# One kernel change: gathering tokens per expert in the first quad of a mixture-of-experts stage

## The chip, the cores and the metric

One core of a Trainium2 chip. The metric is the device time of one execution in microseconds (us), median of several runs. Lower is better.

## The reference, cut to what matters

Two blocks run one after the other on 256 tokens of width 1024, in f32. The first has two hybrid attention layers and is not touched here. The second has two layers, each with an attention and a mixture of experts. Only the experts matter for the change: 32 experts in each layer, and each token goes to two of them.

```python
def hierarchical_moe(h, w_group, b_group, w_expert, b_expert, w_gate, w_up, w_down):
    ...
    def expert_block(args):
        xb, e = args
        return (jax.nn.silu(xb @ w_gate[e]) * (xb @ w_up[e])) @ w_down[e]
    ...
    ys = ys * row_gate[:, None].astype(ys.dtype)
    out = jnp.zeros((N + 1, D), ys.dtype).at[row_tok].add(ys)[:N]
```

`w_gate[e]` and `w_up[e]` are 1024 x 512, `w_down[e]` is 512 x 1024, in f32: 2 MB each, 192 MB in a layer. Every expert's weights are read from memory once.

## The kernel before, in words

**Stages.** The program runs two hybrid layers, then for i = 0 and 1 an attention (`neighbourhood` or `grouped`), the router and the experts of layer i. Each engine has its own instruction list, and they meet at semaphores. Two names say how PSUM's eight banks are handed over: `filled(...)` is raised by TensorE (PE) when a result stands in a bank, `drained(...)` by the engine that has read it. PE's `begin(b, ...)` waits until the last result in bank b is drained.

**The router.** VectorE (DVE) works out the groups, the experts, the position of each token within its expert (`R_PM`) and the gate values. `select(i, q)` (line 1580) builds the 0/1 matrices `SEL` that say which token stands in which of the 32 places of each of the four experts of quad q. After `select(i, 0)` DVE writes the gate values (`gates`), the overflow mask and the counts (lines 1644 to 1653), and then reads one or two results of the conditioning projection (`extract`, lines 1654 and 1655).

**The experts.** 32 experts are eight quads of four, `for q in range(NQ)`. In each quad:
- `gather(q)`: the tokens of all four experts are gathered by matmuls. The stationary operand is a 128 x 128 block of the normalized tokens `XH`, the moving operand is `SEL` of the quad, 128 columns (4 experts x 32 places). There are 8 blocks of columns x 2 blocks of tokens = 16 matmuls, which the trace records as 32 (each f32 matmul has two records). Banks 0 and 1 take the results, and ScalarE (ACT, bank 0) and DVE (bank 1) write them, scaled and shifted, to `XG`. `gather(0)` stands ahead of the loop, `gather(q + 1)` after the last expert of quad q.
- for each expert j of the quad (lines 889 to 915) the gate product (m = 0) and the up product (m = 1), 64 records each with a 128 x 32 block of `XG` as the stationary operand, four of them side by side in the array (line 898). Then ACT takes silu of the gate, DVE multiplies by up (`AA`), PE transposes the product (`hidden(j)`, bank 4) and DVE copies it to `AT`. `hidden(j - 1)` stands after expert j, `hidden(3)` after the loop.
- after expert 0 only (the others leave with `continue`): DVE multiplies `SEL` by `gates` to `GS`, PE transposes that in bank 4 (`gsT`, line 911), DVE copies it to `GST` (line 1707), and builds the next quad's `SEL`. In layer 1, quad 0, `second_gates(i, 1)` (line 667 on PE) follows.
- `down(0)` and `down(1)` (line 932): 64 records each of 128 x 512; then `combine` (line 942) adds the quad's rows to the output with `GST`.

**The weights.** All weights pass through nine slots of 2 MB (`ring` has five, `AR` four). `plan()` assigns every piece to a slot; `PIECE` holds a piece's slot and how often the slot was filled, `BEFORE` the piece that was there. SyncE (SP) issues the loads in the order of use, at line 2325, each after the old piece's `DONE`: the gate product's last matmul for a gate piece, the up product's for an up piece, and `filled("dn", i, q, 1)`, the end of `down(1)`, for a down piece. By the plan, the first down piece of quad 0 (`("dn", i, 0, 0)`) takes slot 7; the other three take the slots of expert 0's gate, expert 0's up and expert 1's gate; the next five pieces (gate and up of experts 4 and 5, gate of expert 6) take those of expert 1's up to expert 3's up. The piece after them, expert 6's up, takes slot 7, and so waits for quad 0's `down(1)`. SP's list is in order: all later loads stand behind it.

**GpSimd (POOL)** adds the layer norm's rows to `X` (`finish`, line 2186), beside the first experts.

Of the kernel before, what the change touches and what calls it, by code (L numbers as in the profile page):

```python
# [130 lines left out]
def program(nc, A, out):  # L131
    with ExitStack() as ctx:
# [175 lines left out]

        def plan():
            age, held, holds, now = list(range(RING + EXTRA)), [0] * (RING + EXTRA), {}, [RING + EXTRA]  # L310

            def put(name, among, at=None):
                s = min(range(among), key=lambda i: age[i])
                age[s] = now[0] if at is None else at
                now[0] += at is None
                held[s] += 1
                PIECE[name], BEFORE[name] = (s, held[s]), holds.get(s)
                holds[s] = name

            n_ada = itertools.count()  # L320
            for l in range(DEPTH):
                for f in LOADS[l]:
                    if f == "ada":
                        put(("ada", next(n_ada)), RING)
                    else:
                        put(("out", l, f) if f in (0, 1) else ("in", l, f), RING)
            for *f, when in NA_LOADS:
                put(("wo", 0, f[1]) if f[0] == "wo" else ("ada", f[1]) if f[0] == "ada" else ("qkv", 0, *f), RING, when)
            for k, when in enumerate((486, 487, 510, 505)):
                age[RING + k] = when  # L330
            now[0] = 1000
            for i in range(DEPTH):
                if i:
                    base = now[0]
                    for *f, when in GQA_LOADS:
                        put(("ada", f[1]) if f[0] == "ada" else ("wo", 1, f[1]) if f[0] == "wo" else ("qkv", 1, *f), RING, base + when)
                    for k, when in enumerate((95, 96, 128, 122)):
                        age[RING + k] = base + when
                    now[0] = base + 200
                for q in range(NQ):  # L340
                    for j in range(4):
                        for m in range(2):
                            put(("gu", i, 4 * q + j, m), RING + EXTRA)
                    for k in down_pieces(q):
                        put(("dn", i, q, *k), RING + EXTRA)
# [68 lines left out]
        def _(eng):  # L414
# [453 lines left out]
            def experts(i):  # L868
                def gather(q):
                    for b in range(2):  # L870
                        o = begin(b, "xg", i, q, b)
# [8 lines left out]
                gather(0)  # L880
                for q in range(NQ):
# [7 lines left out]
                    for j in range(4):  # L889
                        o = begin(2 + j % 2, "gu", i, q, j)  # L890
                        for m in range(2):
# [3 lines left out]
                            for c in range(NC):  # L895
                                pe.wait_ge(*drained("xg", i, q, c // 4))
                                for f in range(4):
                                    ins = eng.matmul(o[32 * f:32 * f + 32, 128 * m:128 * m + 128],  # L898
                                                     XG[u][:, c, 32 * j:32 * j + 32], w[:, c, f::4],
                                                     start=c == 0, stop=c == NC - 1)  # L900
                            if not m:
                                DONE[name] = pe.step(ins)
                        end(ins, "gu", i, q, j)
                        DONE[name] = filled("gu", i, q, j)
                        if j:
                            hidden(j - 1)
                            continue
                        o = begin(4, "gsT", i, q)
                        pe.wait_ge(sem("gs"), 8 * i + q + 1)
                        for t in range(NT):  # L910
                            ins = turn(o[:, 128 * t:128 * t + 128], GS[u][:, t, :])
                        end(ins, "gsT", i, q)
                        if i and not q:
                            second_gates(i, 1)
# [98 lines left out]
        def _(eng):  # L1013
# [575 lines left out]
            def router(i):  # L1589
# [53 lines left out]
                select(i, 0)  # L1643
                for t in range(NT):
                    v.step(tt(gates[:, t, :].rearrange("p (g e) -> p g e", g=4), bcast(ohg[:, t, :], 2, 8),
                              bcast(oh1[:, t, :], 1, 4), ALU.mult))
                v.chain()
                v.step(stt(over[:, :, :], pm, CAP + 0.5, gates[:, :, :], ALU.is_gt, ALU.mult))
# [5 lines left out]
                for n in (23,) if i else (18, 19):  # L1654
                    extract(n)

            def experts(i):
# [15 lines left out]
                gather(0)  # L1673
                for q in range(NQ):
# [8 lines left out]
                    for j in range(4):  # L1683
                        w = j % 2
                        bk = bank("gu", i, q, j)
                        v.wait_ge(*filled("gu", i, q, j))
# [6 lines left out]
                        if j:  # L1693
                            hidden(j - 1)
                            continue
# [10 lines left out]
                        v.wait_ge(*filled("gsT", i, q))  # L1706
                        free(eng.tensor_copy(GST[u], bank("gsT", i, q)[:, 0:256]), "gsT", i, q)
                        if q + 1 < NQ:
                            select(i, q + 1)
                    hidden(3)  # L1710
# [106 lines left out]
            for i in range(DEPTH):  # L1817
# [4 lines left out]
                router(i)  # L1822
                experts(i)
# [3 lines left out]
        def _(eng):  # L1827
# [293 lines left out]
            def experts(i):  # L2121
                def gather(q):
# [13 lines left out]
                gather(0)  # L2136
                for q in range(NQ):
                    for j in range(4):
                        n = 32 * i + 4 * q + j
# [6 lines left out]
                        if i and not (q or j):  # L2146
                            second_gates(i, 1)
# [169 lines left out]
        def _(eng):  # L2317
            sp = Engine(eng, sem("sp"))

            def load(dst, src, *name):  # L2320
                held = BEFORE[name]
                if held:
                    sp.wait_ge(*DONE[held])
                s, _ = PIECE[name]
# [192 lines left out]
```

## Time and profile before

| | us |
|---|---|
| runs shown (three) | 1564.13, 1565.1, 1570.44 |
| median | 1565.1 |
| profiled execution, its time | 1563.89 |
| profiled execution, its span (first to last instruction) | 1562.2 |
| PE busy | 1389.6 (89%) |
| DVE busy | 571.8 (37%) |
| ACT busy | 215.0 (14%) |
| POOL busy | 88.4 (6%) |
| moved by DMA | 533.32 MB |

The span is 1.7 us shorter than the profiled execution's own time. PE is the TensorE matmul row and PEld its weight loads, which overlap it; a busy PE is not a PE at its peak. "PEclk" is the TensorE clock that was granted, as a share of 2.4 GHz, and "DMA" the mean busy share of the core's 16 DMA engines. The expert stage of layer 0 runs from 484 to 942 us of the span, that of layer 1 from 1093 to 1551 us.

### The profile page before, as it was taken

The page shows a single profiled execution, that of the slowest core. Times are in us where ns is not written, and L with a number is a line of the kernel's source. Part 1 is how long each engine was busy: PE and PEld are TensorE (multiplying, and loading weights), DVE is VectorE, ACT ScalarE, POOL GpSimd, SP SyncE. Part 2 cuts the span into 40 slices and gives each one's busy share as a digit, 9 for nine tenths or more (in the row PEclk, how much of TensorE's full clock was granted, in tenths as well). Part 3 has the DMA queues.
Part 4 walks back from the last instruction along what each step waited for, and adds up shares of the span by engine and source line. Part 5 has one row for each costly group of instructions (what it writes and reads, how often), then busy time and mean ns, then how long its engine had stood idle before and what let it go on. Part 6 is the DMA issues. An engine that isn't in the chain of part 4 may idle for free.

```text
span 1562.2 us, 28408 instructions
## 1 busy us (share of the span) xinstructions
PE 1389.6 (89%) x12800; PEld 883.6 (57%) x12800; DVE 571.8 (37%) x1254; ACT 215.0 (14%) x574; POOL 88.4 (6%) x95
## 2 busy tenths in 40 slices
PE   7999999999998999779879788878999797897795
PEld 4885478578886556346446344457655453463451
DVE  3696469655745111101101115684222011011013
ACT  2230123022332000000000002442100000000000
POOL 3100111000003000000000001100200000000000
PEclk9999999999999999889899898999999998998997
DMA  9656845768768999999999998257999999999995
GB/s 345 216 197 233 291 164 198 275 220 288 280 278 340 411 426 426 428 426 426 427 426 428 427 376 320 89 201 282 374 413 426 428 426 427 427 426 427 425 415 201
DMA packets 96856, 533.32 MB, mean 341 GB/s; under 512 B 5184, under 2 KB 7424, under 8 KB 73168
## 3 DMA queue, kind: packets, MB, share of 16 engines
q1 hardware_dynamic: 92992, 519.40, 82.6%
q0 software_dynamic: 3728, 11.95, 2.2%
q8 instruction: 105, 1.72, 0.4%
q14 instruction: 31, 0.25, 0.0%
HBM read 530.28 MB, written 1.05 MB: 340 GB/s over the span
## 4 chain that ended last, share of the span: by engine, by line
PE 65%; DMA 24%; DVE 4%; SPq 4%; ACT 1%; issue 1%; DVEq 0%; ACTq 0%
PE bk L433 28%; PE bk L898 16%; DMA ring<-in_moe_w_down 15%; DMA AR<-in_moe_w_down 9%; PE bk L932 8%; PE bk L614 4%; PE bk L942 4%; SPq L2325 3%; PE bk L429 3%; DVE AR L1017 2%; PE bk L643 1%; PE bk L658 1%; ACT AR L1831 1%; DMA ring<-in_w_in 1%; DVE AR L1025 0%
## 5 line engine op out<-in xcount | busy, mean ns | idle before, releaser
L898 PE MATMUL bk<-ring,AR 128*32 128x128 f32 x4480 | 268.6, 409 | 0.1
L1017 DVE TENSOR_TENSOR AR<-bk,AR 128x128 f32<-128x128 f32 (+2 forms) x106 | 41.3, 390 | 521.6 <-ACT AR L1831 455.6
L898 PE MATMUL bk<-AR 128*32 128x128 f32 x3712 | 223.0, 409 | 0.0
L898 PEld LDWEIGHTS bk<-ring,AR 128*32 128x32 f32 x4480 | 175.7, 127 | 80.9 <-DVE X L1017 4.5
L433 PE MATMUL bk<-ring,AR 128*128 128x256 f32 (+2 forms) x736 | 214.1, 449 | 6.3 <-ACT AR L1831 2.6
L932 PE MATMUL bk<-ring,AR 128*32 128x512 f32 x608 | 159.4, 704 | 51.9 <-DMA ring<-in_moe_w_down 51.1
L1831 ACT ACTIVATE AR<-bk 128x512 f32<-128x512 f32 (+4 forms) x178 | 72.1, 422 | 948.2 <-PE bk L898 774.1
L898 PEld LDWEIGHTS bk<-AR 128*32 128x32 f32 x3712 | 145.5, 127 | 68.5 <-DVE X L1017 4.5
L433 PEld LDWEIGHTS bk<-ring,AR 128*128 128x128 f32 x736 | 140.9, 194 | 73.7 <-issue 56.6
L932 PE MATMUL bk<-AR 128*32 128x512 f32 x416 | 150.9, 709 | 27.8 <-DMA AR<-in_moe_w_down 27.8
L433 PE MATMUL bk<-AR,ring 128*128 128x256 f32 (+1 forms) x832 | 170.5, 364 | 1.7 <-DVE AR L1022 1.4
L433 PEld LDWEIGHTS bk<-AR,ring 128*128 128x128 f32 x832 | 147.5, 190 | 21.6 <-issue 3.4
L932 PEld LDWEIGHTS bk<-ring,AR 128*32 128x32 f32 x608 | 35.4, 126 | 130.1 <-DMA ring<-in_moe_w_down 71.6
L1017 DVE TENSOR_TENSOR AR<-bk,mpart 128x512 f32<-128x512 f32 x32 | 22.1, 692 | 220.9 <-PE bk L932 220.9
L429 PE MATMUL bk<-cst,AR 128*128 128x128 f32 (+1 forms) x356 | 63.9, 293 | 41.5 <-DVE AR L1017 24.1
L1025 DVE SCALAR_TENSOR_TENSOR mpart<-ring,ccol,mpart 128x512 f32<-128x512 f32 x126 | 98.7, 784 | 4.5
L429 PEld LDWEIGHTS bk<-cst,AR 128*128 128x128 f32 (+1 forms) x356 | 41.6, 143 | 79.7 <-issue 55.8
L932 PEld LDWEIGHTS bk<-AR 128*32 128x32 f32 x416 | 32.0, 126 | 73.4 <-DMA AR<-in_moe_w_down 39.7
L433 PE MATMUL bk<-AR 128*128 128x128 f32 (+1 forms) x536 | 72.1, 295 | 0.2
L433 PEld LDWEIGHTS bk<-AR 128*128 128x128 f32 x536 | 67.1, 202 | 4.4 <-issue 2.3
L942 PE MATMUL bk<-AR 128*128 128x512 f32 x128 | 59.7, 606 | 3.3 <-DVE AR L1017 3.3
L1017 DVE TENSOR_TENSOR X<-X,bk 128x512 f32<-128x512 f32 x64 | 44.0, 688 | 40.1 <-PE bk L614 23.9
(152 smaller groups left out, 954.1 us busy)
## 6 DMA issues: line engine op xcount, KB each, us to landing
ring<-in_moe_w_gate SPq DMA_DIRECT2D x36, 2048.0 KB, 28.6
ring<-in_moe_w_up SPq DMA_DIRECT2D x34, 2048.0 KB, 25.0
ring<-in_moe_w_down SPq DMA_DIRECT2D x34, 2048.0 KB, 33.6
AR<-in_moe_w_up SPq DMA_DIRECT2D x30, 2048.0 KB, 29.9
AR<-in_moe_w_gate SPq DMA_DIRECT2D x28, 2048.0 KB, 26.3
ring<-in_ada_w SPq DMA_DIRECT2D x24, 2048.0 KB, 11.0
AR<-in_moe_w_down SPq DMA_DIRECT2D x22, 2048.0 KB, 33.6
ring<-in_w_in SPq DMA_DIRECT2D x12, 2048.0 KB, 12.6
```

The lines of the kernel that those rows point to most:

```text
L429: return eng.transpose(o, a, ident[0:k, 0:k])
L433: ins = eng.matmul(o, l, r, start=i == 0, stop=i == len(pairs) - 1)
L614: ins = eng.matmul(o[:, :], BIG[:, x, OUTS[m] + 128 * t:OUTS[m] + 128 * t + 128], w[:, 2 * m + x, :], start=k + x == 0, stop=k + x == 4)
L643: ins = eng.matmul(o[b][:, a * nk:(a + 1) * nk], g["q"][h][:, t * 128:(t + 1) * 128], g["k"][h][:, 0:nk], start=True, stop=True)
L658: ins = eng.matmul(o[64 * b:64 * b + 64, 128 * x:128 * x + 128], g["v"][2 * x + b][kt], ET[j % 2][:, (2 * b + x) * nkt + kt, :], start=kt ...
L898: ins = eng.matmul(o[32 * f:32 * f + 32, 128 * m:128 * m + 128], XG[u][:, c, 32 * j:32 * j + 32], w[:, c, f::4], start=c == 0, stop=c == N ...
L932: ins = eng.matmul(o[32 * j:32 * j + 32, :], AT[u][:, j, 32 * f:32 * f + 32], w, start=f == 0, stop=f == 3)
L942: end(eng.matmul(o[:, :], GST[u][:, 128 * t:128 * t + 128], YS[:, 512 * n:512 * n + 512], start=True, stop=True), "cb", i, q, n, t)
L1017: return eng.tensor_tensor(o, a, b, op)
L1025: return eng.scalar_tensor_tensor(out=o, in0=a, scalar=s, in1=b, op0=op0, op1=op1)
L1831: return eng.activation(o, a, f, **kw)
L2325: eng.dma_start(dst, src).then_inc(sem(f"slot{s}"), 16)
```

## The change

In quad 0 of each layer every expert's tokens are gathered by themselves: `gather(0, n)` runs the same 16 matmuls with the 32 columns of `SEL` that belong to expert n. `gather(0, 0)` stands ahead of the loop, `gather(0, j + 1)` between expert j's gate and up products. ACT and DVE empty the banks with `gather_first(n)`, 32 columns wide. DVE's end of the router (gates, overflow mask, counts) becomes `router_end`, and runs after `gather_first(0)`.

The load that refills the slot of the first gate piece (it brings the down weights of expert 1) is issued as two loads of 1 MB: the first after half of the gate product (semaphore `half`), the second after all of it.

In all quads, the product of `SEL` and `gates`, and the next quad's `select`, move on DVE from after expert 0 to after expert 2, and the transpose `gsT`, its copy and `second_gates(i, 1)` from after expert 0 to after expert 3. `extract` moves from the router to quad 0, after expert 2.

```diff
@@ plan()
+        def first_gate(name):
+            return name in [("gu", i, 0, 0) for i in range(DEPTH)]
...
-                held[s] += 1
-                PIECE[name], BEFORE[name] = (s, held[s]), holds.get(s)
+                BEFORE[name] = holds.get(s)
+                held[s] += 2 if first_gate(BEFORE[name]) else 1
+                PIECE[name] = s, held[s]
@@ PE, experts(i)
-                def gather(q):
+
+                def gather(q, n=None):
                     for b in range(2):
+                        if n is not None:
+                            o = begin(b, "xe", i, n, b)
+                            pe.wait_ge(sem("xn"), 4 * i + 2)
+                            pe.wait_ge(sem("sel"), 8 * i + 1)
+                            for cc in range(4):
+                                ins = product(o[:, 32 * cc:32 * cc + 32],
+                                              [(XH[:, t, 128 * (4 * b + cc):128 * (4 * b + cc) + 128],
+                                                SEL[0][t][:, n, :]) for t in range(NT)])
+                            end(ins, "xe", i, n, b)
+                            continue
...
-                gather(0)
+                gather(0, 0)
...
-                                pe.wait_ge(*drained("xg", i, q, c // 4))
+                                pe.wait_ge(*(drained("xg", i, q, c // 4) if q else drained("xe", i, j, c // 4)))
...
+                                if first_gate(name) and c == NC // 2 - 1:
+                                    ins.then_inc(sem("half"), 1)
                             if not m:
                                 DONE[name] = pe.step(ins)
+                                if not q and j < 3:
+                                    gather(0, j + 1)
...
                         if j:
                             hidden(j - 1)
-                            continue
-                        o = begin(4, "gsT", i, q)
...
-                        if i and not q:
-                            second_gates(i, 1)
+                    o = begin(4, "gsT", i, q)
+                    pe.wait_ge(sem("gs"), 8 * i + q + 1)
...
+                    if i and not q:
+                        second_gates(i, 1)
                     hidden(3)
@@ DVE, router(i) and experts(i)
                 select(i, 0)
+                return ohg, oh1
+            def router_end(i, ohg, oh1):
...
+                def gather_first(n):
+                    v.wait_ge(*filled("xe", i, n, 1))
+                    for cc in range(4):
+                        c = 4 + cc
+                        ins = ts(XG[0][:, c, 32 * n:32 * n + 32], bank("xe", i, n, 1)[:, 32 * cc:32 * cc + 32],
+                                 COMB[:, 2 * i, 0, c:c + 1], ALU.mult, COMB[:, 2 * i, 1, c:c + 1], ALU.add)
...
-                gather(0)
+                gather_first(0)
+                router_end(i, *chosen)
...
+                        if not q and j < 3:
+                            gather_first(j + 1)
...
+                        if j != 2:
                             continue
...
-                        v.wait_ge(*filled("gsT", i, q))
-                        free(eng.tensor_copy(GST[u], bank("gsT", i, q)[:, 0:256]), "gsT", i, q)
                         if q + 1 < NQ:
                             select(i, q + 1)
+                        if not q:
+                            for n in (23,) if i else (18, 19):
+                                extract(n)
+                    v.wait_ge(*filled("gsT", i, q))
+                    free(eng.tensor_copy(GST[u], bank("gsT", i, q)[:, 0:256]), "gsT", i, q)
                     hidden(3)
@@ ACT, experts(i)
-                gather(0)
+                gather_first(0)
...
+                        if not q and j < 3:
+                            gather_first(j + 1)
...
-                        if i and not (q or j):
-                            second_gates(i, 1)
+                    if i and not q:
+                        second_gates(i, 1)
@@ SP, load(dst, src, *name)
+                if first_gate(held):
+                    h = dst.shape[1] // 2
+                    sp.wait_ge(sem("half"), held[1] + 1)
+                    eng.dma_start(dst[:, 0:h, :], src[:, 0:h, :]).then_inc(sem(f"slot{s}"), 16)
+                    sp.wait_ge(*DONE[held])
+                    eng.dma_start(dst[:, h:2 * h, :], src[:, h:2 * h, :]).then_inc(sem(f"slot{s}"), 16)
+                    return
```

## Rows read from the trace of the kernel before

**Rows 1.** Stretches: us, busy us of engines (instructions), then PEclk, DMA share, GB/s.
```profile
540.00:580.00 40.00, 37.99 (x570) 24.63 (x566) 5.33 (x18) 2.62 (x8) 0.00 (x0) 1.00 1.01 427
...
1150.00:1500.00 350.00, 302.22 (x3800) 172.88 (x3796) 52.67 (x138) 15.68 (x48) 0.59 (x1) 0.94 1.01 427
```

**Rows 2.** PE's waits in layer 0's experts: us in total, times, longest.
```profile
PE bk L932 <- DMA ring<-in_moe_w_down: 21.7, 7, 4.8
```

**Rows 3.** Order of time, DMA issues of SP in layer 0: start, us, engine, line.
```profile
493.68 10.40 SPq L2325 DMA_DIRECT2D ring<-in_moe_w_down  x3
...
522.96 0.33 SPq L2325 DMA_DIRECT2D AR<-in_moe_w_gate  x1
534.85 0.33 SPq L2325 DMA_DIRECT2D AR<-in_moe_w_up  x1
```

**Rows 4.** Stretches of 1 us around the restarts of DMA (columns as in 1).
```profile
492.00:493.00 1.00, 1.00 (x24) 0.69 (x20) 0.00 (x0) 0.00 (x0) 0.00 (x0) 1.00 0.02 8
...
535.00:536.00 1.00, 1.00 (x3) 0.40 (x3) 0.67 (x2) 0.00 (x0) 0.00 (x0) 1.00 0.88 262
536.00:537.00 1.00, 1.00 (x4) 0.41 (x3) 0.83 (x2) 0.00 (x0) 0.00 (x0) 1.00 0.72 229
...
1145.00:1146.00 1.00, 1.00 (x4) 0.49 (x3) 0.83 (x2) 0.00 (x0) 0.00 (x0) 1.00 0.43 147
```

**Rows 5.** Order of time: quad 1's gather, and the `down` after it.
```profile
524.05 3.74 PE L433 MATMUL bk<-AR 128*128 128x128 f32 x32
...
527.72 0.62 PE L932 MATMUL bk<-AR 128*32 128x512 f32 x1
```

**Rows 6.** Order of time: router logits, 36 moving columns, and the last record's length.
```profile
474.73 1.95 PE L433 MATMUL bk<-wr,AR 128*128 128x36 f32 x16
L433 PE MATMUL bk<-wr,AR x16: 271/279/279, 474.7 to 476.4; 128*128 128x36 f32 x16
```

**Rows 7.** Low clock: 32-column matmuls, the first gather, and the stretch in layer 0.
```profile
482.49 1.47 PE L433 MATMUL bk<-AR,ones 128*128 128x32 f32 x6
484.04 5.72 PE L433 MATMUL bk<-AR 128*128 128x128 f32 x32
481.00:488.00 7.00, 6.30 (x28) 6.20 (x29) 6.41 (x25) 0.61 (x4) 0.00 (x0) 0.52 1.02 410
```

**Rows 8.** Order of time, layer 0: expert 0, the `gsT` stop, expert 1.
```profile
489.70 7.59 PE L898 MATMUL bk<-ring,AR 128*32 128x128 f32 x128
...
499.50 0.41 PE L429 MATMUL bk<-cst,AR 128*128 128x128 f32 x2 [2.21 <-DVE AR L1017]
499.84 3.87 PE L898 MATMUL bk<-ring,AR 128*32 128x128 f32 x64
499.95 0.42 DVE L1707 COPY AR<-bk 128x256 f32<-128x256 f32 x1 [0.59 <-PE bk L429]
...
503.50 3.96 PE L898 MATMUL bk<-AR 128*32 128x128 f32 x64
```

**Rows 9.** The same place in layer 1.
```profile
1097.87 7.62 PE L898 MATMUL bk<-ring,AR 128*32 128x128 f32 x128
...
1107.32 0.41 PE L429 MATMUL bk<-cst,AR 128*128 128x128 f32 x2 [1.82 <-DVE AR L1017]
1108.71 3.88 PE L898 MATMUL bk<-ring,AR 128*32 128x128 f32 x64
```

**Rows 10.** Order of time, layer 0: the transpose after expert 3.
```profile
523.89 0.33 PE L429 MATMUL bk<-cst,AR 128*128 128x128 f32 x1 [0.74 <-DVE AR L1681]
```

**Rows 11.** Order of time: readers of the banks, and POOL beside them.
```profile
487.83 1.50 ACT L1831 ACTIVATE AR<-bk,cst 128x128 f32<-128x128 f32 x4 [5.76 <-PE bk L433]
493.15 5.85 POOL L2186 TENSOR_TENSOR X<-AR 128x1024 f32<-128x1024 f32 x2 [17.66 <-DMA AR<-in_ln_g]
497.75 0.29 DVE L1017 TENSOR_TENSOR AR<-bk,AR 128x128 f32<-128x128 f32 x1 [6.57 <-ACT AR L1831]
500.29 3.89 DVE L1017 TENSOR_TENSOR AR<-cst,AR 128x128 f32<-128x128 f32 x2
```

More of the change, by code:

```diff
@@ L906, in experts @@
                             hidden(j - 1)
-                            continue
-                        o = begin(4, "gsT", i, q)
[L909 to L912, printed above, removed]
-                        if i and not q:
-                            second_gates(i, 1)
+                    o = begin(4, "gsT", i, q)
+                    pe.wait_ge(sem("gs"), 8 * i + q + 1)
+                    for t in range(NT):
+                        ins = turn(o[:, 128 * t:128 * t + 128], GS[u][:, t, :])
+                    end(ins, "gsT", i, q)
+                    if i and not q:
+                        second_gates(i, 1)
                     hidden(3)
@@ L1647, in router @@
                 v.chain()
-                v.step(stt(over[:, :, :], pm, CAP + 0.5, gates[:, :, :], ALU.is_gt, ALU.mult))
+                v.step(stt(over[:, :, :], R_PM, CAP + 0.5, gates[:, :, :], ALU.is_gt, ALU.mult))
                 v.wait_ge(*filled("ct", i))
@@ L1653, in router, with experts @@
                 v.tell(eng.tensor_copy(cnt[:, NE:NE + 1], rt(388, 1)), sem("cnt"), i + 1)
-                for n in (23,) if i else (18, 19):
-                    extract(n)
-            def experts(i):
+            def experts(i, chosen):
+                def gather_first(n):
[4 more added lines that the diff above has]
+                                 COMB[:, 2 * i, 0, c:c + 1], ALU.mult, COMB[:, 2 * i, 1, c:c + 1], ALU.add)
+                        if cc == 3:
+                            free(ins, "xe", i, n, 1)
+                        else:
+                            v.step(ins)
                 def gather(q):
@@ L1821, in _ @@
                     neighbourhood()
-                router(i)
-                experts(i)
+                experts(i, router(i))
                 last_norm(i)
@@ L2121, in experts, with gather_first @@
             def experts(i):
+                def gather_first(n):
+                    s.wait_ge(*filled("xe", i, n, 0))
+                    for c in range(4):
+                        ins = act(XG[0][:, c, 32 * n:32 * n + 32], bank("xe", i, n, 0)[:, 32 * c:32 * c + 32], ACT.Identity,
+                                  bias=COMB[:, 2 * i, 1, c:c + 1], scale=COMB[:, 2 * i, 0, c:c + 1])
+                        if c == 3:
+                            free(ins, "xe", i, n, 0)
+                        else:
+                            s.step(ins)
                 def gather(q):
@@ L2321, in load @@
                 held = BEFORE[name]
+                s, _ = PIECE[name]
+                if first_gate(held):
[5 more added lines that the diff above has]
+                    return
                 if held:
                     sp.wait_ge(*DONE[held])
-                s, _ = PIECE[name]
                 eng.dma_start(dst, src).then_inc(sem(f"slot{s}"), 16)
```

## The prediction

> **What bounds the kernel now.** I read the stretches first. From 540 us on, with one exception per layer, the DMA engines are busy all of the time in the expert stages, at 427 GB/s [rows 1]. A stage whose loads run without a break ends when the last of them has landed, so what one edit is worth is: by how much does it move the moment from which the loads run without a break? The waits say the same from the other side: in layer 0's experts PE's longest sums of waits are `down` matmuls waiting for their weights (seven waits of 21.7 us in all on one kind of slot) [rows 2]. They are PE's slack, and no slack of the loads.
>
> The unbroken run begins late. SP's issues [rows 3] show why: expert 6's up goes to slot 7, which holds the first down piece, so its load (issued at 534.85) waits for quad 0's `down(1)`, and everything behind it in SP's list waits too. The issue before it was at 522.96. The loads queued by then had landed: 535 to 537 us moved 262 and 229 GB/s instead of 427, and layer 1 has the same hole at 1145 [rows 4]. There is an earlier hole at 492, where SP waits for the first gate's slot [rows 4], but only eight more pieces may be issued before `down(1)` ends, and they have all but landed when it does; filling that hole alone moves nothing. So the stage of each layer hangs on PE's list from the first gather to the end of quad 0's `down(1)`: what PE gains or loses there, the layer gains or loses. PE does not wait for a load in it.
>
> **The gathers.** Before, quad 0 has one gather of 32 records; after, four of 32 records each, since the 16 blocks of `XH` are loaded into the array for each expert anew and only the moving side shrinks, from 128 columns to 32. What does a record with few columns cost? In quad 1's gather the records come (3.74 - 0.28) / 31 = 0.112 us apart with 128 columns, and from its start to that of the next `down` it is 3.67 us [rows 5]. The router's logits have the same 128 x 128 stationary block and 36 columns: (1.95 - 0.28) / 15 = 0.111 us apart [rows 6]. So the spacing does not depend on the columns here, and a gather of 32 columns costs what one of 128 does. At the lower clock (granted 0.52 in that stretch, that is mostly 1.2 GHz) 32-column matmuls lie (1.47 - 0.40) / 5 = 0.214 us apart [rows 7] (0.40 is the length of one), twice as much. I take 3.67 us for each of the three added gathers, 11.0 us in each layer, because the nearest row is 36 columns wide and agrees. Bounds: 32 x 0.106 = 3.4 us if the spacing falls a little with the 4 columns fewer and the seam costs nothing (5% under the row of 36, my allowance), and 32 x 0.214 = 6.8 us if it runs wholly at 1.2 GHz.
>
> The rule of the Trainium skill, TensorE: Matmul & The Clock Gate, section "Back-to-back issue gap", would speak against this: it gives some 60 cycles (25 ns) for 1 to 64 columns. By it alone a 32-record gather would be 0.8 us. The same page's section "LDWEIGHTS (loading the stationary operand)" gives columns / 1.2 ns for the weight load, 107 ns for 128 columns, which the 0.111 us agree with. The first rule is a rival below.
>
> The first gather (5.72 us, from 484.04) [rows 7] is followed by expert 0 without a gap, at 489.70 [rows 8]. `gather(0, 0)` has as many loads at the same clock, so expert 0 starts when it did: 0. Bound: if the clock rises later than before, up to 32 x 0.214 + 0.3 - 5.72 = +1.4 us; downward 0.3 us. The bank readers get narrower, but they were hidden behind PE's own gather already.
>
> **The `gsT` stop.** Layer 0: expert 0's two products start 3.66 us apart (503.50 - 499.84, as for expert 1), so PE could start expert 1 at 489.70 + 7.32 = 497.02, and starts it at 499.84: 2.8 us, of which 2.21 are the wait for DVE's `GS` [rows 8]. They go: nothing stands between expert 0 and 1 any more. Layer 1: 1097.87 + 7.32 = 1105.19 against 1108.71: 3.5 us, with the second gates in it [rows 9].
>
> They come back in part after expert 3. PE waits there for DVE to copy the transpose of expert 2 before it may transpose expert 3, at 523.89 (0.74 us of wait) [rows 10]; all of these use bank 4. Now `gsT` takes that turn: from its start to the end of its copy 499.95 + 0.42 - 499.50 = 0.87 us [rows 8], some 0.9 with the hand-over, and only then expert 3's transpose. +0.9 us in layer 0. In layer 1 `second_gates` follows it, 1108.71 - 1107.32 = 1.4 us [rows 9]; its copy is within that: +1.4 us. Behind the transpose wait the next gather and both downs. In quads 1 to 7 the same move is a gain of under 1 us for PE, in a stretch in which the loads decide: 0.
>
> **What has cover.** `gather_first(j + 1)` on ACT and DVE runs while PE does expert j's up product, 3.66 us. ACT's four reads of 128 columns took 1.50 us [rows 11], at 32 they take no more. DVE's place beside POOL matters: two products of two SBUF operands took 3.89 us while POOL was at work, but one that reads a bank 0.29 us in the same time [rows 11]. `gather_first` reads a bank, so 0; if it were slowed like the others, 4 x 1.95 = 7.8 us less the 3.66 of cover and the 1.8 in which the next gate uses ACT's half: up to +2.3 us. `router_end` and `extract` move into DVE's idle time (DVE is at 5 of 40 us in such a stretch [rows 1]); nobody waits for them before `gsT`. If PE were faster there, `gs` would be next to be late. For SP: the halved load is issued about 1.9 us earlier in its first half, and the second when the whole was before; what is queued behind it (down weights of experts 2 and 3, quad 1's gates) waits for PE anyway. All of those come later, by one gather each up to three, and still land before PE needs them: expert 6's gate is issued near 531 and quad 0's `down` starts near 537. Worth 0, since not the hole before but `down(1)` decides. The select and `GS` products move out of POOL's way, which only DVE feels.
>
> **The sum.** Layer 0: 11.0 - 2.8 + 0.9 = +9.1 us. Layer 1: 11.0 - 3.5 + 1.4 = +8.9 us. Together +18.0. The profiled execution took 1563.9 us: 1581.9. The median of the runs shown is 1.2 us above it, less than the spread of the three; I predict 1582, 1.1% slower. With the small bounds (per layer 3 x 0.27 and 0.3 less; 1.4 at the start and 2.3 for DVE more) this case alone spans 1580 to 1589.
>
> **Rivals.**
> - The clock. In layer 0 PE's granted clock was mostly 1.2 GHz from 481 to 488, through the router's small matmuls and most of the first gather, after PE had waited for the router [rows 7]. It had risen when expert 0 ran. If the gathers within quad 0 run at 1.2 GHz, each costs 32 x (0.214 - 0.112) = 3.3 us more: one per layer 1588.5, all three 1602. For it: no row shows the clock holding through several gathers of few columns. Against: the logits with 36 columns ran at 0.111 us a record [rows 6], half of the low clock's 0.214, and in quad 0 PE has no more waits than before. Chance 0.14.
> - The columns decide (not slower). Place: the four gathers. Price: a quarter, 3.67 / 4 = 0.9 us each. Then the first gather ends some 4 us earlier, of which 3.5 reach expert 0 after ACT's reads; layer 0 comes to -3.5 + 2.8 - 2.8 + 0.9 = -2.6 us, layer 1 to about -2.2 (a first gather shorter by 0.5): 1559. It turns from loss to gain below some 0.05 us a record (3p - 1.9 less 3.5 x (3.67 - p) / 2.75 is nil at p = 1.5 us). With the earlier first loads also counting it could reach 1553, and this is the only way to over 0.5% faster. For it is only that 32 is under 36; the spacing at 36 is against it. By the skill's issue gap the same sum holds with 0.8 in place of 0.9. Chance 0.09, of which 0.03 beyond 0.5%.
> - The loads absorb it (no change). PE waits tens of us for weights in quads 2 to 7 [rows 2], so 9 us more in quad 0 might vanish there. Then 1565, with the gain at `gsT` perhaps 1562. Against: those waits follow the loads, and the loads start their unbroken run 9 us later with as many bytes to move. It holds only if the loads had a reserve, such as a backlog over quad 0's end; the holes at 535 and 1145 say that there is none. Chance 0.07.
>
> **How the numbers follow.** Forecast 0.70, clock 0.14, columns 0.09, absorbed 0.07. About 0.5%, 8 us, is what a measurement of this kernel can tell from no change. Slower by more than that: forecast, clock, 0.84 less 0.01 for a sum that comes out at half: 0.83. Same: 0.06 + 0.07 + 0.01 = 0.14. Faster 0.03. The range 1573 to 1595 holds the forecast, its bounds and those of DVE beside POOL, and the clock's cases up to about one and a half gathers a layer; it leaves out the two rivals without a loss and three slow gathers.
>
> **What would show it.** Right: in quad 0 of each layer three new groups of 32 records of `bk<-AR`, 128x32, each near 3.6 us, between gate and up; expert 1 starts straight after expert 0's up; `down(1)` of quad 0 ends near 544 us instead of 535; the DMA hole ahead of it grows from 1 to some 8 us (with smaller ones between the earlier pieces), and then 427 GB/s as before; the stage of each layer ends 9 us later. The clock rival would show groups of 6 to 7 us; the column rival groups near 1 us and expert 0 starting near 486; the absorbed one a DMA without a longer hole. I am wrong if the records lie closer than 0.1 us, or if the loads' rate after the hole is not the same.

## The result, and the profile after

The changed kernel takes 1586.19 us (four runs, 1585.17 to 1587.12) against 1565.71 us before (1564.13 to 1570.44): 20.5 us more, ratio 1.0126, 95% interval 1.0103 to 1.0148. Forecast were 1582 us, between 1573 and 1595. Timed again beside the experiments, on another chip, the same kernel took 1582.47 us against 1564.74 (ratio 1.0115, 1.0085 to 1.0144), so the size of the loss is 18 to 21 us.

| | before | after |
|---|---|---|
| profiled execution, its time | 1563.89 | 1586.37 |
| its span | 1562.2 | 1584.5 |
| PE busy | 1389.6 | 1421.4 |
| PE instructions | 12800 | 12992 |
| first gather to SP's restart (end of quad 0's `down(1)`), layer 0 | 50.8 | 62.4 |
| the same, layer 1 | 50.9 | 62.1 |
| restart in layer 1 to the end of the span | 418.6 | 418.6 |

The last three rows of the table are differences of start times in the traces: of before 534.85 - 484.04 [rows 3, 7] in layer 0, 1143.65 - 1092.76 and 1562.2 - 1143.65 in layer 1. PE has 192 records more, 2 x 3 x 32.

Below is PE's order of time in the profile after, layer 0 and then the first gather of layer 1 (start, us, engine, line and operation, operands, records, idle time before it). Line 439 is the gather's, line 915 the gate and up products, line 435 the transposes. Of before, [rows 7, 8] answer to the upper part and [rows 10] to the transpose at 537.36.

```profile
485.90 7.00 PE L439 MATMUL bk<-AR 128*128 128x32 f32 x32 [0.26 <-DVE AR L1037]
492.84 3.87 PE L915 MATMUL bk<-ring,AR 128*32 128x128 f32 x64
496.64 3.76 PE L439 MATMUL bk<-AR 128*128 128x32 f32 x32
500.33 7.51 PE L915 MATMUL bk<-ring,AR 128*32 128x128 f32 x128
507.77 3.76 PE L439 MATMUL bk<-AR 128*128 128x32 f32 x32
511.46 3.88 PE L915 MATMUL bk<-AR 128*32 128x128 f32 x64
...
519.32 4.53 PE L439 MATMUL bk<-AR 128*128 128x32 f32 x32
...
535.36 0.33 PE L435 MATMUL bk<-cst,AR 128*128 128x128 f32 x1
536.40 0.44 PE L435 MATMUL bk<-cst,AR 128*128 128x128 f32 x2 [0.72 <-DVE AR L1715]
537.36 0.33 PE L435 MATMUL bk<-cst,AR 128*128 128x128 f32 x1 [0.52 <-DVE AR L1749]
...
1103.86 7.00 PE L439 MATMUL bk<-AR 128*128 128x32 f32 x32
```

Expert 0's up and expert 1's gate are one unbroken group now (500.33, 128 records): the `gsT` stop is gone. Three gathers stand in the quad, 3.69 us from the start of one to the next matmul (500.33 - 496.64, 511.46 - 507.77) and 4.46 for the third. After expert 3, `gsT` at 536.40 and the copy it waits for put expert 3's transpose at 537.36, 2.00 us after expert 2's; before it was 1.07 (from 522.82 to 523.89, the latter in [rows 10]).

The next fence holds SP's issues in the order of time after, layer 0 (of before [rows 3]), and stretches of 1 us around the restart (columns as in [rows 1]; of before [rows 4]).

```profile
494.93 0.33 SPq L2377 DMA_DIRECT2D ring<-in_moe_w_down  x1
496.76 0.33 SPq L2379 DMA_DIRECT2D ring<-in_moe_w_down  x1
504.22 4.00 SPq L2383 DMA_DIRECT2D ring<-in_moe_w_down  x2
...
535.47 0.33 SPq L2383 DMA_DIRECT2D AR<-in_moe_w_gate  x1
548.33 0.33 SPq L2383 DMA_DIRECT2D AR<-in_moe_w_up  x1
...
545.00:546.00 1.00, 1.00 (x16) 0.32 (x12) 0.59 (x1) 0.00 (x0) 0.00 (x0) 1.00 0.18 66
547.00:548.00 1.00, 1.00 (x12) 0.13 (x4) 0.00 (x0) 0.00 (x0) 0.00 (x0) 1.00 0.00 0
548.00:549.00 1.00, 1.00 (x6) 0.49 (x3) 0.67 (x1) 0.00 (x0) 0.00 (x0) 1.00 0.00 0
...
1172.00:1500.00 328.00, 286.79 (x3626) 167.56 (x3618) 48.50 (x132) 15.69 (x48) 0.59 (x1) 0.93 1.01 426
```

The reader is to see the hole: from 545 to 549 us the DMA engines move next to nothing, while PE is busy with the downs. The load at 548.33 ends it, and from then on the rate is 426 GB/s with no break, as before. PE's waits for down weights in layer 0's experts are 39.6 us instead of 38.7 before (of which [rows 2] show one line), 20.6 and 19.0 in the two kinds of slot:

```profile
PE bk L952 <- DMA ring<-in_moe_w_down: 20.6, 8, 4.7
PE bk L952 <- DMA AR<-in_moe_w_down: 19.0, 6, 4.2
```

PE's waits for weights did not shrink with the added work; the loads and PE moved together.

### The profile page after: what moved, and what is told of

Same layout as the page of the kernel before. It is cut to its first block, busy times and chain, and to the rows that moved or that the text cites. A ratio compares the mean times of both kernels' runs of the same rounds, so it can differ in the third digit from the quotient of the medians.

```text
span 1584.5 us, 28846 instructions
## 1 busy us (share of the span) xinstructions
PE 1421.4 (90%) x12992; PEld 913.0 (58%) x12992; DVE 568.1 (36%) x1278; ACT 221.2 (14%) x598; POOL 87.8 (6%) x95
## 4 chain that ended last, share of the span: by engine, by line
PE 66%; DMA 25%; DVE 4%; SPq 3%; ACT 1%; issue 1%; DVEq 0%; ACTq 0%
PE bk L439 29%; PE bk L915 16%; DMA ring<-in_moe_w_down 15%; DMA AR<-in_moe_w_down 9%; PE bk L952 8%; PE bk L620 3%; PE bk L962 3%; SPq L2383 3%; PE bk L435 2%; PE bk L649 1%; PE bk L664 1%; DVE AR L1037 1%; ACT AR L1870 1%; DMA ring<-in_w_in 1%; DVE sm L1048 0%
## 5 line engine op out<-in xcount | busy, mean ns | idle before, releaser
L952 PE MATMUL bk<-ring,AR 128*32 128x512 f32 x608 | 164.4, 718 | 50.3 <-DMA ring<-in_moe_w_down 49.5
L952 PE MATMUL bk<-AR 128*32 128x512 f32 x416 | 154.9, 726 | 29.7 <-DMA AR<-in_moe_w_down 29.6
L439 PE MATMUL bk<-AR 128*128 128x128 f32 (+2 forms) x728 | 98.6, 296 | 0.3 <-DVE AR L1037 0.3
L439 PEld LDWEIGHTS bk<-AR 128*128 128x128 f32 x728 | 92.9, 207 | 7.2 <-issue 5.1
L435 PE MATMUL bk<-cst,AR 128*128 128x128 f32 (+1 forms) x356 | 64.6, 295 | 27.2 <-DVE AR L1715 11.6
L1042 DVE TENSOR_SCALAR AR<-bk,cst 128x128 f32<-128x128 f32 (+1 forms) x88 | 26.9, 367 | 99.5 <-PE bk L439 99.5
```

Of the source, the lines that this page charges most:

```text
L435: return eng.transpose(o, a, ident[0:k, 0:k])
L439: ins = eng.matmul(o, l, r, start=i == 0, stop=i == len(pairs) - 1)
L952: ins = eng.matmul(o[32 * j:32 * j + 32, :], AT[u][:, j, 32 * f:32 * f + 32], w, start=f == 0, stop=f == 3)
L1042: return eng.tensor_scalar(o, a, s1, s2, op0, op1)
```

## The experiments

All times are medians beside the kernel before on the same chip. The times of single runs differ by some microseconds (the kernel before took 1560.4 to 1573.6 us beside the second set), so where a term of 2 us matters I read it in the trace, between the first gather and SP's restart. One trace is no exact measure of it either: in the profile of `x_q3` below these two stretches are 52.9 and 53.6 us, 4.7 us more in sum than before, though its edit touches nothing in quad 0. There the first gathers took 6.55 and 6.26 us, and PE waited 3.42 us for `GS` in both layers, where it was 2.21 and 1.82 before.

### Three idle gathers in quad 0, and the same in quad 3

```diff
 if not m:
     DONE[name] = pe.step(ins)
+    if q == 0 and j < 3:          # the other kernel: q == 3
+        o2 = begin(5, "idle", i, j)
+        for b in range(2):
+            for cc in range(4):
+                ins2 = product(o2[:, 128 * cc:128 * cc + 128],
+                               [(XH[:, t, 128 * (4 * b + cc):128 * (4 * b + cc) + 128],
+                                 SEL[q % 2][t].rearrange("p e s -> p (e s)")) for t in range(NT)])
+        end(ins2, "idle", i, j)
```

> The kernel before with three idle gathers of 32 records (128 moving columns, results unused, bank 5) in quad 0, between the gate and up products of experts 0, 1 and 2; nothing else changed. Output is the reference's. Theory (quad 0's PE list decides): 3 x 3.7 = 11.0 us in each layer, 22 us in all, near 1588. Rival (the later quads' slack absorbs it): 1566.

Measured: 1583.23 us against 1565.83, ratio 1.0122 (1.0086 to 1.0157), 17.4 us more. The 22 us expected lie within this interval. The first gather and the restart of each layer, PE's and SP's order of time:

```profile
480.44 5.92 PE L433 MATMUL bk<-AR 128*128 128x128 f32 x32
543.88 0.33 SPq L2336 DMA_DIRECT2D AR<-in_moe_w_up  x1
...
1096.67 6.67 PE L433 MATMUL bk<-AR 128*128 128x128 f32 x32
1160.36 0.33 SPq L2336 DMA_DIRECT2D AR<-in_moe_w_up  x1
```

That is 63.4 and 63.7 us instead of 50.8 and 50.9, 25.4 more in sum, and from the last restart to the end it is 418.2 us (span 1578.6) as before. The span still grew by 16.4 only: the first gather began 3.6 us earlier than before, and the stretch from layer 0's restart to layer 1's first gather was 5.1 us shorter, both outside the edit.

> The same three idle gathers in quad 3 instead of quad 0, at the same places. Theory: the loads run without a break by then and PE waits over 5 us per quad for down weights, so the 11 us in each layer are taken out of these waits as far as they reach (some 6 to 8 us within the quad, the rest within the next), and the loads do not stop: between 1566 and 1570. Rival (any added PE time in the experts counts in full): 1588.

Measured: 1565.65 us against 1565.83, ratio 0.9993 (0.9974 to 1.0012).

The same 96 records a layer at the same places of a quad cost 17 us in quad 0 and nothing that can be seen in quad 3. This is the sharpest test of the main step, that a layer hangs on PE's list up to quad 0's `down(1)`. Where did the work in quad 3 go? The first stretch is quad 3's end in layer 0 of the kernel before, the second the same stretch with the idle gathers in that quad (columns as in [rows 1]); then the longest sums of PE's waits around it, before and with them.

```profile
684.00:704.00 20.00, 12.70 (x65) 2.90 (x64) 2.00 (x6) 0.00 (x0) 0.00 (x0) 0.74 1.01 428
```

```profile
684.00:704.00 20.00, 19.27 (x249) 11.54 (x243) 3.33 (x10) 2.06 (x6) 0.00 (x0) 1.00 1.01 428
```

```profile
PE bk L932 <- DMA ring<-in_moe_w_down: 7.3, 2, 3.8
```

```profile
PE bk L429 <- DVE AR L1025: 1.3, 1, 1.3
```

The wait of 7.3 us for down weights is gone, and the granted clock in that stretch is 1.00 instead of 0.74: the downs no longer start after a pause of PE. From the first `down` of the quad to `combine` it is 703.70 - 683.64 = 20.1 us before and 705.17 - 698.17 = 7.0 us with the idle gathers. These 13.1 us, 7.3 of waits and the rest of low clock, took in the 3 x 3.77 = 11.3 us of added work. The DMA row is the same, 428 GB/s, in both.

### Columns or stationary blocks

```diff
 # a_wide: every per-expert gather with all columns
-ins = product(o[:, 32 * cc:32 * cc + 32], [(XH[...], SEL[0][t][:, n, :]) for t in range(NT)])
+ins = product(o[:, 128 * cc:128 * cc + 128], [(XH[...], SEL[0][t].rearrange("p e s -> p (e s)")) for t in range(NT)])
 # a_pair: expert 0, then experts 1 to 3 at once
+k = 3 if n else 1
+ins = product(o[:, 32 * k * cc:32 * k * cc + 32 * k], [(XH[...], SEL[0][t][:, n:n + k, :]...) for t in range(NT)])
...
-if not q and j < 3:
+if not q and j < 1:
     gather(0, j + 1)
```

> The changed kernel, with every per-expert gather done with all 128 moving columns of SEL (the readers take the 32 that belong to the expert). Same number of matmuls, four times the columns. Theory (the stationary blocks set the spacing): each of the three gathers inside quad 0 stays at 3.7 us. The first gather tells what kept the clock low: if it is that 32 columns are little work, it takes 5.7 us in layer 0 and 5.2 in layer 1 as before the change instead of 6.9, and the kernel is 3 us under the changed one, near 1583; if the late rise was chance, 1586. Rival (columns decide): the gathers get longer by up to 2.8 us each, over 16 us in all, above 1600.

Measured: 1581.02 us, ratio 1.0107 to before (1.0086 to 1.0128). From this kernel's order of time in layer 0, the first gather and the first of the added ones:

```profile
482.11 5.96 PE L439 MATMUL bk<-AR 128*128 128x128 f32 x32
...
491.78 3.84 PE L439 MATMUL bk<-AR 128*128 128x128 f32 x32
495.55 7.54 PE L915 MATMUL bk<-ring,AR 128*32 128x128 f32 x128
```

Four times the columns, and it lasts 3.77 us to the next matmul (495.55 - 491.78) against 3.69. Up to 128 columns they don't decide. Above that they do: in layer 1's attention of the changed kernel 32 records with 256 columns, at a granted clock of 1.00, lie 0.22 us apart instead of 0.11.

```profile
1084.39 7.15 PE L439 MATMUL bk<-ring,AR 128*128 128x256 f32 x32
```

The first gathers of `a_wide` took 5.96 us in layer 0 (5.7 expected) and 6.53 in layer 1, not the 5.2 expected, but both less than 7.0. The kernel is near the 1583 us that were expected for the width; the width of the first gather is taken up below.

> The changed kernel with two gathers in quad 0 instead of four: expert 0 alone, then experts 1 to 3 in one gather (96 moving columns) between expert 0's gate and up. Theory: each gather that is left out is worth its 3.7 us in each layer whatever its columns, so 4 x 3.7 = 14.8 us less than the changed kernel, near 1571. Rival (columns decide): the same columns are moved, so the time stays at 1586. Rival (absorbed): the time doesn't follow the number of gathers.

Measured: 1569.60 us, ratio 1.0025 to before (1.0011 to 1.0040); against the changed kernel 16.6 us less by its first timing and 12.9 by its second (1582.47), around the 14.8 expected. Two gathers fewer in each layer, with the same columns moved:

```profile
480.58 7.01 PE L439 MATMUL bk<-AR 128*128 128x32 f32 x32
487.52 3.93 PE L916 MATMUL bk<-ring,AR 128*32 128x128 f32 x64
491.38 4.03 PE L439 MATMUL bk<-AR 128*128 128x96 f32 x32
```

### The clock under the first gather

The forecast took the first gather as unchanged. In the traces it lasts 7.00 or 7.01 us in both layers of the changed kernel and of `a_pair`, and 5.17 to 6.67 us in the kernels in which it has 128 columns. Two more runs ask whether that goes with the width.

```diff
 # a_mix: expert 0's gather with all columns, the other three as they are
+k = 1 if n else 4
 for cc in range(4):
-    ins = product(o[:, 32 * cc:32 * cc + 32], [(XH[...], SEL[0][t][:, n, :]) ...])
+    ins = product(o[:, 32 * k * cc:32 * k * cc + 32 * k], [(XH[...], SEL[0][t][:, n:n + k, :]...) ...])
```

> The changed kernel with only the first gather, the one ahead of expert 0, done with all 128 moving columns; the three inside quad 0 keep 32. So far the first gather took 7.0 us in the changed kernel, in both layers, and in the run with experts 1 to 3 in one gather, both with 32 columns, and 5.2 to 6.7 us in all runs with 128. If the width holds the clock down there: 5.2 to 6.7 us here in both layers, and 0.6 to 3.6 us less in all than the changed kernel, near 1584. If the four 7.0 us were chance: 7.0 again in one of the layers at least, 1586.

Measured: 1580.93 us, ratio 1.0101 (1.0071 to 1.0130). Its first gathers:

```profile
482.54 6.00 PE L439 MATMUL bk<-AR 128*128 128x128 f32 x32 [0.32 <-DVE AR L1038]
...
1099.49 6.41 PE L439 MATMUL bk<-AR 128*128 128x128 f32 x32
```

> The changed kernel as it is, beside the run before on the same chip. All theories: 1586, 7.0 us for the first gather in both layers if its width holds the clock down. From the end of quad 0's down(1) in layer 1 to the end of the program 418.5 us, as in all runs in which the loads had drained by then.

Measured: 1582.47 us, ratio 1.0115 (1.0085 to 1.0144); first gathers 7.01 and 7.00 us; 1578.7 - 1160.36 = 418.3 us from the restart to the end.

The first fence holds the changed kernel (its first profile): both first gathers as stretches, then the third inner gather of layer 0. The second holds the same two places of the kernel before (columns as in [rows 1]; the granted clock is the third figure from the end).

```profile
485.90:492.80 6.90, 6.90 (x32) 6.87 (x32) 0.00 (x0) 1.18 (x4) 0.00 (x0) 0.50 0.96 405
1103.90:1110.80 6.90, 6.90 (x33) 6.83 (x33) 0.00 (x0) 1.18 (x4) 0.00 (x0) 0.50 0.99 416
519.30:523.80 4.50, 4.50 (x40) 4.42 (x36) 0.00 (x0) 1.18 (x4) 0.00 (x0) 0.81 0.95 371
```

```profile
484.00:489.70 5.70, 5.66 (x33) 5.57 (x33) 4.29 (x10) 1.85 (x5) 0.00 (x0) 0.64 1.01 415
1092.80:1097.90 5.10, 5.10 (x36) 4.98 (x37) 1.28 (x6) 1.69 (x5) 0.00 (x0) 0.72 0.98 412
```

With 32 columns the granted clock is 0.50, 1.2 GHz, through the whole first gather; with 128 it rises within it. In all traces of this study: 7.00 or 7.01 us in six of six first gathers with 32 columns, 5.17 to 6.67 us in twenty of twenty with 128. Against the changed kernel `a_mix` has nothing but this width changed (and where its readers look in the bank), so the late rise follows from it here. In the trace the stretches from first gather to restart are 61.4 and 61.7 us in `a_mix` and 62.9 and 62.1 in `a_same`. In total time the effect is small: `a_mix` is 1.5 us under the changed kernel on the same chip, and the intervals overlap, so only the trace shows it.

### The parts of the change without its gathers

```diff
 # b_gst: the kernel before, only the gs/gsT/second_gates move (as in the change)
 # b_half: the kernel before, only first_gate(), sem("half") and the load in two halves (as in the change)
 # b_both: the two together
```

> The kernel before with only one part of the change: the product of SEL and gates and the next select behind expert 2, gsT, its copy and the second gates behind expert 3, in all quads. No added gather, no halved load. Theory (a layer's stage hangs on the end of quad 0's down(1)): that end comes 2.8 - 0.9 = 1.9 us earlier in layer 0 and 3.5 - 1.4 = 2.1 us earlier in layer 1, the loads restart that much earlier, and the kernel takes 4.0 us less, near 1561.7. If PE's slack in the later quads decides instead (absorbed), the kernel takes as long as before, 1565.7, although down(1) ends earlier. If the loads queued ahead of the restart decide, the gain is at most the hole of about 1 us in each layer: 1563.7.

Measured: 1557.86 us, ratio 0.9953 (0.9935 to 0.9971), 7.7 us less.

> The kernel before with only the first gate slot's refill in halves. Theory: no change, 1565.7: the hole at 492 us gets shorter by up to 2 us and the one at 535 us longer by as much, since the restart there waits for down(1). Rival (each hole of the loads counts): 2 us in each layer less, 1561.7.

Measured: 1566.49 us against 1565.83, ratio 0.9999 (0.9976 to 1.0023): nothing. The rival's 4 us less would be a ratio of 0.9974, just outside.

> As the run before, and with the first gate slot's refill in halves too: the change without its per-expert gathers. Theory: the halved load fills a part of the hole at 492 us and moves the end of nothing, so the time is that of the move alone, 4.0 us under before, near 1561.7. If the hole at 492 counts by itself, some 2 us in each layer more: near 1558. Either way the part of the change that costs is the gathers: against the changed kernel (1586.2) this one should be 24 us shorter.

Measured: 1560.76 us, ratio 0.9966 (0.9952 to 0.9980), 4.8 us less, and 22 to 25 us under the changed kernel. So the move of `gsT` gains, the halves bring nothing that can be seen on top, and what costs is the gathers.

The size for `b_gst` is above the 4.0 us expected, whose ratio of 0.9974 lies just outside its interval and inside that of `b_both`. In the profiles the time from the first gather to the restart is 49.2 and 49.0 us in the two layers of `b_both` against 50.8 and 50.9: the expected 1.9 and 2.1 less, within half a microsecond. In `b_gst` it is 49.2 and 51.6; in the latter layer the gather of quad 1 ran partly at the low clock:

```profile
1085.96 6.22 PE L433 MATMUL bk<-AR 128*128 128x128 f32 x32
...
1125.13 5.37 PE L433 MATMUL bk<-AR 128*128 128x128 f32 x32
```

Of the 6.4 us by which the span of this profile is shorter (1555.8), only 0.9 lie between first gather and restart in the two layers. 1.5 us lie ahead of the first gather (482.58 instead of 484.04) and 3.8 between layer 0's restart and layer 1's first gather (554.2 against 557.9). These 3.8 lie behind the experts: from the restart to layer 0's last `combine` it is 405.8 us against 405.4, and from there to layer 1's first gather 148.4 against 152.5. That last stretch, the attention and router of layer 1, is 148.1 to 152.5 us in the thirteen profiles, and the kernel before is its longest. The stop at `gsT` isn't of one length either: in the kernels that have it in its old place PE waits 1.6 to 3.4 us for `GS`, and a longer stop is worth more to remove. Whether one of these makes up what the median shows over 4 us is not shown, and I leave it open.

### Getting `down(1)` out of the way

```diff
 hidden(3)
-if q + 1 < NQ:
+if q and q + 1 < NQ:
     gather(q + 1)
...
     down(1)
+    if not q:
+        gather(1)
     combine(0)
```

The same on DVE; with the moved `gsT`, and once with and once without the halves.

> The kernel before with gsT moved and the halved refill, and in quad 0 the gather of quad 1 placed behind down(1) instead of ahead of down(0), on PE and DVE. Theory: down(1) of quad 0 ends 3.7 us earlier again, 5.6 to 5.8 us in all; the loads queued ahead (8 x 4.9 us from about 493 us) are then the bound, landing near 533 us, so the restart comes 3 to 4 us earlier than before in each layer: 1557.7 to 1560, provided the gather's readers stay covered by the combine of quad 0 (3.6 us). If down(1) alone decides: 11.4 us less, 1554.3.

Measured: 1558.74 us against 1565.83, ratio 0.9953 (0.9933 to 0.9974), 7.1 us less.

> The kernel with gsT moved and quad 1's gather behind down(1), but with the first gate slot refilled whole, not in halves. In the version with halves the loads never stopped at quad 0's end in layer 0 (no hole at 528 us), so there the loads queued before decide and an earlier first load should count. Theory: without the halves the loads begin about 1.8 us later in each layer and end as much later: up to 3.6 us more than with them (1558.7), so near 1561 to 1562. Rival (the halved load is worth nothing anywhere, as alone in the kernel before): 1558.7.

Measured: 1555.86 us against 1564.74, ratio 0.9947 (0.9929 to 0.9965), 8.9 us less. My expectation of a loss without the halves fell: the medians go the other way, and the intervals overlap. The profiles show what the step before it said, though. First SP's issues around quad 0's end with the halves, in layer 0, and the stretches there:

```profile
517.39 0.33 SPq L2342 DMA_DIRECT2D AR<-in_moe_w_gate  x1
527.15 0.33 SPq L2342 DMA_DIRECT2D AR<-in_moe_w_up  x1
...
526.00:527.00 1.00, 1.00 (x12) 0.16 (x4) 0.00 (x0) 0.00 (x0) 0.00 (x0) 1.00 1.06 442
527.00:528.00 1.00, 1.00 (x12) 0.97 (x9) 0.69 (x1) 0.00 (x0) 0.00 (x0) 1.00 0.95 393
528.00:529.00 1.00, 1.00 (x11) 1.00 (x10) 0.00 (x0) 0.00 (x0) 0.00 (x0) 1.00 1.00 426
```

There is no hole any more in layer 0: the restart comes 46.2 us after the first gather's start (527.15 - 480.93) and the loads queued before it are still running. What was gained ahead of the restart was lost behind it: against `b_both` it comes 2.9 us sooner after the first gather (46.2 against 49.2), and from it to layer 0's last `combine` it is 409.0 us instead of 405.2. So `down(1)` has stopped being the bound in this layer, and 3.7 us more from it brought little: 1558.7, within the 1557.7 to 1560 expected, against 1560.8 and 1557.9 of the two versions with the gather in its old place. Of these versions `b_late_whole` has the lowest median; its interval and those of `b_gst` and `b_late` overlap, so I can only say that all three beat both kernels, by 0.5%.

## Why the prediction was right

**What bounds.** Held. A restart that comes later moves the end of the stage by as much. The time from the restart in layer 1 to the end of the span is 418.2 to 418.8 us in the kernels before and after, `b_gst`, `b_half`, `a_wide`, `a_pair`, `a_mix`, `a_same` and `x_q0`, although these spans reach from 1555.8 to 1584.5 us. It is 419.2 in `x_q3` with 11 us of work more in it, and 419.3 and 422.1 in the two versions in which the loads had not drained at the restart. `b_both` alone is outside this pattern, at 421.0, which takes back in its profile what the earlier restart gained in layer 1, and I have no cause for it. In layer 0 the time from the restart to the last `combine` is 405.4 us before and 405.0 after, and 404.7 to 407.4 in the eleven profiles in which the loads had drained. `x_q0` against `x_q3` shows the rest.

**The price of a gather.** Held: 11.0 us for three was forecast; measured 3.69 + 3.69 + 4.46 = 11.8 in layer 0 and 3.69 x 3 = 11.1 in layer 1. The choice that mattered was to take the row of 36 columns for 32 [rows 6]. Of the two rules of the Trainium skill, TensorE: Matmul & The Clock Gate, that of "LDWEIGHTS (loading the stationary operand)" agrees with the traces here: 107 ns by the page, and 3.69 us for 32 records, 0.115, measured. The 25 ns of its table in "Back-to-back issue gap" did not show. That section gives the table for a single matmul by itself, and says that in a stream of weight loads and matmuls both set the spacing; the prediction quotes the row without this. Every matmul record here has a weight load of its own (12992 of each in the page of the profile), and `a_wide` shows that fewer columns than 128 gain nothing; that it is the loads that set the spacing is argued from this and not tested, for no run keeps its stationary block. The products ahead of the added gathers also got longer: 496.64 - 492.84 = 3.80 us instead of 3.66, about 0.4 us a layer for the three, which the sum did not have.

**The `gsT` stop and its return.** Held. The stop is gone (500.33, one group of 128), and after expert 3 it costs 2.00 - 1.07 = 0.93 us in layer 0, forecast 0.9; in layer 1 expert 2's transpose starts at 1152.47 and expert 3's at 1154.95, 2.48 us, 1.4 more than 1.07, forecast 1.4.

**The first gather.** This is the term that was mis-sized. I took 0 with a bound of +1.4, worked out for layer 0. The time from its start to expert 0's is 492.84 - 485.90 = 6.94 us instead of 5.66, +1.3, and in layer 1 1110.80 - 1103.86 = 6.94 instead of 5.11, +1.8, above the bound. With the low clock in one inner gather of layer 0 (+0.8) these are 3.9 us of clock. The step that failed was "as many loads at the same clock": the loads were as many, but the clock rose only after them. My clock rival had the right mechanism, in a small dose and mostly at the gather that I had taken as unchanged.

**The sum.** First gather to restart: forecast +9.1 and +8.9, measured +11.6 and +11.2, together 22.8. The span grew by 22.3. In layer 0 the first gather also began 1.9 us later than before; its cause lies ahead of the experts, where the edit changes nothing, and the stretch between the restart of layer 0 and the first gather of layer 1 was 2.4 us shorter (1103.86 - 548.33 = 555.5 against 557.9). The two cancel. Of the 2.4 us, 2.0 lie behind layer 0's last `combine`, where nothing was changed either. The first gather began between 480.4 and 485.9 us in the thirteen profiles of this study, and the stretch was 552.8 to 558.7 us in the eleven of them in which the loads had drained. The medians differ by 17.7 and 20.5 us. That the first of these is so near to my 18.0 is in part luck, for in the profile of that timing (`a_same`) the two stretches are 23.3 us longer than before, more than I had summed.

**The holes.** The hole before the restart grew from 1 us to some 4.5, less than the 8 I gave, because there were also longer ones earlier: the second half of the first load was issued at 496.76 and the next load only at 504.22, after the gather between gate and up. Which of the holes is how long does not matter to the end. `b_half` shows it from the other side: 1.8 us earlier for the first load, nothing to be seen at the end. `down(1)` ended at 548.3 and not near 544: +1.9 from ahead of the experts, +2.1 from the clock.

**The rivals.** Columns: excluded by `a_wide` and `a_pair`. Absorbed: excluded for quad 0 by `x_q0`, and it is what happens in quad 3. That the readers of the banks become late beside POOL: not seen; the four reads of `gather_first(1)` on DVE, under POOL's work, took 0.97 us, as did those of the later experts without it.

## What to carry to other kernels

Before work is cut into finer pieces on PE, ask which side stays whole. Here a gather for one expert (32 moving columns) cost as much as one for four (128), since the tokens were the stationary side and all their blocks came again. This holds up to the 128 columns measured; with 256 a record took twice as long. In a stage whose loads run without a break, look for the instruction at which the loads last had to restart; only PE time ahead of that moment counts, and time behind it is free until it is as long as the waits. When the loads queued ahead of that restart no longer drain in time, the bound has moved to them.

## What the runs showed of the hardware that was not expected

With 32 moving columns the clock of TensorE stayed at 1.2 GHz through the whole of the first gather (7.0 us, six of six), although PE was busy without a gap; with 128 columns and the same records it rose to 2.4 GHz within it (5.2 to 6.7 us, twenty of twenty). Inner gathers of 32 columns behind an expert's products mostly ran at the full clock: in the two profiles of the changed kernel and that of `a_mix` thirteen of eighteen groups took 3.76 to 3.81 us by the trace (3.69 to the next matmul) and five 3.99 to 4.53. With 128 columns eleven of twelve took 3.84 us (`a_wide`, and quad 0 of `x_q0`) and one 4.20.

A wait in front of the downs goes with a low clock in them: in quad 3 of the kernel before PE waited 7.3 us and the granted clock was 0.74 on the mean of 684 to 704 us; with the wait filled by idle gathers it was 1.00, and 11.3 us of work fitted where 7.3 us of waits and 5.8 us of low clock had been.
